# Expert weights in a ring of 20 pieces, a list of the used experts, and the first matrix in 2 MB transfers: a mixer and mixture-of-experts layer on one core

## The chip, the cores and the metric

The kernel runs on one core of a Trainium2 chip. The metric is the device time of one execution in microseconds (us).

## The reference, cut to what matters

One decoder layer with 512 tokens of width 1024, all in float32. A conditioning vector `c` gives shifts, scales and gates (`w_ada`, 24 MB). The first half of the layer (RG-LRU and pooling heads, `w_in`, `w_out`) gives `x1`. The second half is the mixture of 32 experts, of which each token uses four:

```python
logits = ht @ router_w + router_b
top_val, top_idx = lax.top_k(logits, TOP_K)          # 4 of 32
gates = jax.nn.softmax(top_val, axis=-1)
...
u = xb @ w1[e] + b1[e]                               # xb: the tokens of expert e; w1[e] is 1024 x 2048, 8 MB
y = clamped_swiglu(u) @ w2[e] + b2[e]                # w2[e] is 1024 x 1024, 4 MB
out = out.at[tok].add(y * wt)
```

Then a norm, a gate and the residual. Each used expert costs 12 MB of weights, however few tokens it has.

## The kernel before, in words

The kernel is written for each engine by hand, with semaphores between them. SyncE (SP) issues nearly all loads, ScalarE (ACT) activations and some loads, VectorE (DVE) arithmetic and routing, GpSimd (POOL) the gathers and scatters, TensorE (PE) the products.

**Head.** PE goes through `w_ada` in 24 pieces of 1 MB (`mod_piece`, L1253, three buffers; SP issues them in `load_ada`, L389), with the products of `w_in` (L1293) between them; SP issues the two 2 MB parts of `w_in` (`load_win`) and the 4 MB `w_out` between these pieces. Products with `w_out` are L1335.

**Routing.** DVE ranks the tokens by expert (`route_tile`, then L1074 to L1128) and writes `counts`, four rows of 32 integers in one partition: steps, halves, full steps, and 16 or 0 for whether the expert is loaded. PE makes the table of tokens (L1393). POOL gathers the first tokens from `h_rows` (L580), and PE turns them (L1406).

**Experts.** The tokens of an expert are worked on in halves of 32; a step is up to two halves. A matrix product with 32 tokens uses a quarter of the array's columns, four products at a time. For each expert PE makes the bias product (L1497), then for every half an up product over the 8 pieces of `w1` (`up`, L1418), turns the activations (L1427), then for every half a down product over the 4 pieces of `w2` (`down`, L1446). In the trace each product of float32 has two instructions, so a half's up product is x64 and its down product x32. The last pass over a piece counts up `w1_used` or `w2_used`; `u_ps` and `y_ps` say that the last piece is done.

**Weights.** `W1` has two slots of 8 pieces, `W2` one slot of 4; a piece is 1 MB, 8 KB in each of 128 partitions. SP loads `w1` of expert e into slot e modulo 2 as the up product of e - 2 frees its pieces (`load_w1`, L372). ACT loads `w2` of expert e as the down product of e - 1 frees them (`load_w2`, L377), on its own queue. Expert 0 is loaded ahead, `w1` of expert 1 once the counts are there. Every loop over experts goes over all 32 numbers in order: on PE as 16 rounds over a body written twice (L1485 to L1545). An expert without tokens is branched over (L1489, L1543) and its slot stays unused. In this input one expert has none: it is number 1.

**Tail.** When the last scatter is done (`moe_done`, L648) PE turns the gates (L1551) and multiplies by `b2` (L1563), SP loads the experts' results (`y_rows`, L483), and DVE sums them (L1214, L1217).

Of the kernel before, what the change touches and what calls it, by code (L numbers as in the profile page):

```python
# [5 lines left out]
def hybrid_layer(nc, x, c, w_ada, b_ada, norm_mix_pre, norm_mix_post, w_in, conv_w, conv_b, gate_a_w, gate_a_b,  # L6
# [32 lines left out]
    VECS = 72  # L39

# [9 lines left out]
    w1_v = expert_w1[0].rearrange("e (k p) n -> e p k n", p=P)  # L50
# [3 lines left out]
    with ctx:  # L54
# [10 lines left out]
        W1 = sb("W1", [P, 2, KT, F2])  # L65
        W2 = sb("W2", [P, J, 2, D])
# [29 lines left out]
        def flat(v):  # L96
            return v.rearrange("p a b -> p (a b)")
# [3 lines left out]
        w_out_sb = W2[:, :, :, :].rearrange("p c r n -> p (c r) n")  # L101
        HALF = KT // 2
        A_lo, A_hi = flat(W1[:, 0, 0:HALF, :]), flat(W1[:, 0, HALF:KT, :])
        B_lo, B_hi = flat(W1[:, 1, 0:HALF, :]), flat(W1[:, 1, HALF:KT, :])

# [75 lines left out]
        idx_n = take(NQ).bitcast(i32)  # L181

# [7 lines left out]
        sel_e = take(2, P)  # L190
# [7 lines left out]
        counts = OV[0:1, 6656 - 4 * E:6656].rearrange("p (a e) -> p a e", a=4).bitcast(i32)  # L198

        y_all = carver(flat(W1[:, 1, :, :]))(TT, TOPK, D)  # L200
        take = carver(flat(W1[:, 0, :, :]))
# [87 lines left out]
        w1_in = [sems(f"w1_in{s}_", KT) for s in range(2)]  # L289
        w2_in = sems("w2_in", J)  # L290
# [80 lines left out]
        def load_w1(sp, e, slot, k):  # L371
            sp.dma_start(W1[:, slot, k, :], w1_v[bass.ds(e, 1), :, k, :].rearrange("e p n -> p (e n)"))\  # L372
                .then_inc(w1_in[slot][k], 16)


        def load_w2(engine, e, c, experts=w2_v):
            engine.dma_start(W2[:, c, :, :].rearrange("p r n -> p (r n)"),  # L377
                             experts[bass.ds(e, 1), :, c, :].rearrange("e p n -> p (e n)")).then_inc(w2_in[c], 16)

        @block.sync  # L380
        def _(sp):
# [31 lines left out]
            for k in range(KT):  # L413
                load_w1(sp, 0, 0, k)
            sp.wait_ge(prod, number["mix", TT - 1, 1] + 1)
            for c in range(J):
                load_w2(sp, 0, c)
# [5 lines left out]
            for k in range(KT):  # L423
                sp.sem_inc(w1_in[1][k], 16)
            load = sp.value_load(counts[0:1, 3, 1:2], min_val=0, max_val=16)
            with sp.If(load > 0):
                for k in range(HALF):
                    load_w1(sp, 1, 1, k)
            sp.wait_ge(idx_ok, 1)
            with sp.If(load > 0):  # L430
                for k in range(HALF, KT):
                    load_w1(sp, 1, 1, k)
            step, landed = sp.alloc_register("sp_step"), [sp.alloc_register(f"sp_landed{v}") for v in range(2)]
            sp.reg_mov(step, 0)
            full = sp.alloc_register("sp_full")
            sp.reg_mov(full, 0)
            sp.reg_mov(landed[0], 16)
            sp.reg_mov(landed[1], 16)
            sp.reg_add(landed[1], landed[1], load)

            def add_steps(e):
                n_steps = sp.value_load(counts[0:1, 0, e], min_val=0, max_val=T // (2 * H))
                sp.reg_add(step, step, n_steps)
                n_full = sp.value_load(counts[0:1, 2, e], min_val=0, max_val=T // (2 * H))
                sp.reg_add(full, full, n_full)

            def all_up(s, f):

                sp.wait_ge(u_ps[0], s + 1)
                apart(sp)  # L450
                sp.wait_ge(u_ps[1], f + 1)
                apart(sp)
# [1138 lines left out]
```

## Time and profile before

| what | value |
|---|---|
| median of 3 runs | 1488.22 us (1486.9 to 1490.2) |
| the profiled execution | 1486.98 us |
| its span in the trace | 1485.2 us |
| PE busy | 1235.9 us, 83% |
| data moved | 462.84 MB, 312 GB/s over the span |
| granted TensorE clock, mean | 0.904 |

Times in the trace count from the span's start. PE is TensorE's products, PEld its weight loads, PEq and SPq are sequencers. In a view of windows a row has start and end, length, then for each engine its busy time and the number of its instructions, then the granted clock (1.00 is 2.4 GHz, 0.50 is 1.2 GHz), the share of the DMA engines' time in use, and GB/s; where it is made for one line, only that line's instructions are counted. In a timeline a row has start, length, engine, line and operation; in brackets stand the idle time before it and what ended it. A row of waits has who waited, for whom, us in total, times, longest. In the chain of waits a row has start, length and what ran.

### The profile page before, as it was taken

To read this page: it belongs to the slowest core of one execution; us is meant where nothing else is said; L and a number is where in the kernel's file an instruction comes from. 1 tells how busy PE (TensorE), PEld (TensorE's weight loads), DVE (VectorE), ACT (ScalarE), POOL (GpSimd) and SP (SyncE) were. 2 spreads that over 40 slices of the span, in tenths; PEclk is the share of its full clock that TensorE was granted. 3 is DMA by queue.
4 is the path that set the end of the run, shared out by engine and by line. 5 is a ranking of instruction groups with operands and counts; after the bars stand their busy time and mean duration, and the time that the engine had idled before them with its cause. 6 is when DMAs were issued, how large, how long until landed. Compare 5 with 4: busy or idle time off the path is not lost.

```text
span 1485.2 us, 28342 instructions
## 1 busy us (share of the span) xinstructions
PE 1235.9 (83%) x8843; PEld 419.1 (28%) x8844; DVE 412.6 (28%) x864; ACT 218.8 (15%) x482; POOL 277.9 (19%) x421
## 2 busy tenths in 40 slices
PE   4799996567998999967767999987799889989961
PEld 1334455211332333311112333321132223322320
DVE  3223344411232232221111222321122222222317
ACT  2106632000101111110100111110011001101101
POOL 3023001210222132211110221321021211211212
PEclk9799996787999999987868999997799999999975
DMA  9971514399459678899999980689998998899354
GB/s 323 394 269 53 216 46 198 130 416 387 186 193 422 282 316 328 363 420 420 421 420 419 419 347 10 249 355 419 402 404 363 420 421 328 326 421 421 142 213 185
DMA packets 77461, 462.84 MB, mean 312 GB/s; under 512 B 11924, under 2 KB 12052, under 8 KB 29312
## 3 DMA queue, kind: packets, MB, share of 16 engines
q1 hardware_dynamic: 49280, 314.72, 52.1%
q10 hardware_dynamic: 17568, 126.14, 20.5%
q0 software_dynamic: 10592, 21.72, 4.3%
q8 instruction: 11, 0.18, 0.1%
q14 instruction: 10, 0.08, 0.0%
HBM read 453.08 MB, written 16.91 MB: 316 GB/s over the span
## 4 chain that ended last, share of the span: by engine, by line
PE 67%; DMA 15%; DVE 6%; SPq 5%; ACT 3%; issue 3%; POOLq 1%; ACTq 1%; POOL 0%; DVEq 0%
PE bank L1418 33%; PE bank L1446 18%; DMA W<-in_expert_w 12%; SPq L372 4%; PE bank L1293 4%; PE bank L1335 4%; PE bank L1427 2%; DMA W<-in_w_ada 2%; PE bank L1497 2%; PE bank L1253 1%; PE bank L1406 1%; DVE W L1217 1%; DVE OV L1139 1%; DMA OV<-h_rows,src_cur 1%; DMA W<-y_rows 1%
## 5 line engine op out<-in xcount | busy, mean ns | idle before, releaser
L1418 PE MATMUL bank<-W,OV 128*32 128x512 f32 x5056 | 576.9, 609 | 49.4 <-DMA W<-in_expert_w 49.4
L1446 PE MATMUL bank<-W,OV 128*32 128x512 f32 x2528 | 320.4, 652 | 44.7 <-ACT OV L798 22.1
L1418 PEld LDWEIGHTS bank<-W,OV 128*32 128x32 f32 x5056 | 157.2, 111 | 443.3 <-issue 364.9
L1139 DVE TENSOR_TENSOR OV<-bank,OV 128x512 f32<-128x512 f32 x79 | 54.7, 692 | 489.3 <-PE bank L1418 483.8
L1446 PEld LDWEIGHTS bank<-W,OV 128*32 128x32 f32 x2528 | 83.0, 117 | 227.6 <-issue 191.5
L1152 DVE COPY OV<-bank 64x512 f32<-64x512 f32 x79 | 54.8, 693 | 298.4 <-PE bank L1446 296.1
L580 POOL DMA_INDIRECT OV<-h_rows,src_cur x104 | 106.6, 1025 | 61.8 <-POOL src_cur L575 42.7
L575 POOL COPY src_cur<-OV 128x2 int32 (+1 forms) x52 | 11.5, 222 | 523.3 <-PE bank L1406 493.6
L793 ACT ACTIVATE OV<-OV 128x256 f32<-128x256 f32 x79 | 35.3, 447 | 467.1 <-DVE OV L1141 453.7
L1427 PE MATMUL bank<-ident,store 128*128 128x128 f32 x216 | 49.0, 316 | 48.2 <-DVE store L1147 47.3
L1293 PE MATMUL bank<-W 128*128 128x512 f32 x192 | 86.1, 602 | 0.0
L798 ACT ACTIVATE OV<-bank 128x256 f32<-128x256 f32 x108 | 40.6, 386 | 204.1 <-PE bank L1427 199.6
L1427 PEld LDWEIGHTS bank<-ident,store 128*128 128x128 f32 x216 | 33.4, 205 | 91.9 <-issue 91.8
L1156 DVE TENSOR_TENSOR OV<-bank,OV 64x512 f32<-64x512 f32 x79 | 53.9, 683 | 19.0 <-DMA y_rows<-OV,dst_cur_a 9.8
L1335 PE MATMUL bank<-W,OV 128*128 128x512 f32 x128 | 56.2, 594 | 0.9 <-issue 0.9
L590 POOL DMA_INDIRECT y_rows<-OV,dst_cur_a x51 | 47.5, 930 | 47.7 <-POOL dst_cur_a L586 41.1
L821 ACT ACTIVATE OV<-bank 128x512 f32<-128x512 f32 x31 | 18.5, 598 | 248.6 <-issue 155.8
L789 ACT ACTIVATE OV<-bank 128x256 f32<-128x256 f32 x102 | 35.9, 374 | 122.9 <-PE bank L1406 122.9
L1293 PEld LDWEIGHTS bank<-W 128*128 128x128 f32 x192 | 36.4, 193 | 49.3 <-issue 48.9
L586 POOL COPY dst_cur_a<-OV 64x1 int32 (+1 forms) x51 | 9.2, 180 | 209.2 <-DVE OV L1156 209.2
L1406 PE MATMUL bank<-ident,OV 128*128 128x128 f32 x204 | 34.8, 295 | 12.2 <-DMA OV<-h_rows,src_cur 12.2
L1497 PE MATMUL bank<-b_all,OV 128*128 128x512 f32 x62 | 39.1, 717 | 6.8 <-issue 6.8
(231 smaller groups left out, 681.7 us busy)
## 6 DMA issues: line engine op xcount, KB each, us to landing
W<-in_expert_w SPq DMA_DIRECT2D x252, 1024.0 KB, 16.9
W<-in_expert_w ACTq DMA_DIRECT2D x120, 1024.0 KB
W<-in_w_ada SPq DMA_DIRECT2D x24, 1024.0 KB, 8.4
W<-y_rows SPq DMA_DIRECT2D x4, 2048.0 KB, 14.6
W<-in_w_in SPq DMA_DIRECT2D x3, 2048.0 KB, 11.8
W<-in_w_out SPq DMA_DIRECT2D x1, 4096.0 KB, 25.0
store<-in_x SPq DMA_DIRECT2D x4, 512.0 KB, 5.2
h_rows<-W POOLq DMA_DIRECT2D x4, 512.0 KB, 3.3
```

Of the source, the lines that this page charges most:

```text
L372: sp.dma_start(W1[:, slot, k, :], w1_v[bass.ds(e, 1), :, k, :].rearrange("e p n -> p (e n)"))\
L580: pool.indirect_dma_start(xg[hf], None, h_rows, bass.IndirectOffsetOnAxis(ap=src_cur[:, hf:hf + 1], axis=0), bounds_check=T * J - 1, oob_i ...
L1139: TTo(u_sb[:, hf, :], bank[hf][:, :], b1_cur, ALU.add).then_inc(u_ok[hf], 1)
L1152: nc.vector.tensor_copy(y_part[hf], bank[4 + hf][YP:2 * YP, :]).then_inc(y_part_ok, 1)
L1156: TTo(y_sb[hf], bank[4 + hf][0:YP, :], y_part[hf], ALU.add).then_inc(y_ok[hf], 1)
L1293: last = mm(ps[:, :], win_ring[:, slot, k, f * P:(f + 1) * P], hT[:, k, :], start=(k == 0), stop=(k == KT - 1))
L1335: last = mm(ps[:, :], catT[:, k, i * P:(i + 1) * P], w_out_sb[:, k, n * 512:(n + 1) * 512], start=(k == FT), stop=(k == FT - 1))
L1406: last = tr(bank[2][:, at:at + P], xg[hf][:, m * P:(m + 1) * P], ident[:, :])
L1418: last = mm(bank[hf][H * j:H * j + H, :], xT[:, hf, k % QM, H * (k // QM):H * (k // QM) + H], W1[:, slot, k, UW * j:UW * j + UW], start=(k ...
L1427: last = tr(gT_bank[hf][:, r * P:(r + 1) * P], act_store[:, hf, r::2], ident[:, :])
L1446: last = mm(bank[4 + hf][H * j:H * j + H, :], gT[:, hf, r, H * c:H * c + H], W2[:, c, r, HW * piece:HW * piece + HW], start=(c == 0), stop ...
L1497: mm(b1_bank[:, :], sel_e[:, slot, :], b1_all[:, :], start=True, stop=True).then_inc(b1_ps, 1)
```

## The change

The two buffers become one, `W`, of the same size: five groups of four pieces. The expert at place i of a list takes groups 3i, 3i + 1 and 3i + 2, modulo 5: two for `w1`, one for `w2`. A piece is refilled when the piece that stood in it five groups earlier is used up. All weights are now loaded by SP, in the order in which PE uses them; ACT loads none.

The list holds the experts that have tokens (and expert 0), in order, 36 places. PE, DVE and SP work it out before the table of tokens is made: a product counts each expert's tokens, another gives its place, two more write halves and numbers by place into `counts`. POOL, ACT and DVE go over the places one by one. PE and SP go over them in 7 rounds of a body written five times, so their last round ends with places that hold no expert.

`w1` is read with two neighbouring rows per partition, 16 KB at a time, in four transfers of 2 MB in place of eight of 1 MB; a transfer waits for both of its pieces to be free, and PE waits for both to be there. The turn of the tokens (L1406) reads every second element to match.

Three smaller things: in the head the 4 MB of `w_out` are loaded after the last piece of `w_ada`, and the second part of `w_in` after three more pieces; ACT makes the sigmoid of `c` before the squares of `x`; DVE makes the bias selector of the next expert after this one's activations.

```diff
+    GROUPS = 5
+    NPOS = E + J
+    LAPS = 7
-    w1_v = expert_w1[0].rearrange("e (k p) n -> e p k n", p=P)
+    w1_v = expert_w1[0].rearrange("e (c p r) n -> e p c (r n)", p=P, r=2)
-        W1 = sb("W1", [P, 2, KT, F2])
-        W2 = sb("W2", [P, J, 2, D])
+        W = sb("W", [P, GROUPS, J, F2])
...
+        def load_w1(sp, e, g, k):
+
+            sp.dma_start(W[:, g, k % J:k % J + 2, :].rearrange("p r n -> p (r n)"),
+                         w1_v[bass.ds(e, 1), :, k // 2, :].rearrange("e p n -> p (e n)")).then_inc(w_in_at[g][k % J], 16)
+            sp.sem_inc(w_in_at[g][k % J + 1], 16)
...
+            return [(3 * u + part) % GROUPS for part in range(3)]
...
-            load_win(2, 1)
             for n in range(2 * PIECES, 2 * PIECES + ADA_RING):
                 load_ada(n)
-            sp.dma_start(w_out_sb, w_out_v).then_inc(wout_in, 16)
+            load_win(2, 1)
...
+            sp.dma_start(w_out_sb, w_out_v).then_inc(wout_in, 16)
...
+            def first_matrix(e, u, uses):
+
+                g = groups_of(u)
...
+                for k in range(0, KT, 2):
+                    part, c = k // J, k % J
+                    landed_there(g[part], c, uses[part])
+                    landed_there(g[part], c + 1, uses[part])
+                    if k + 1 < J - 1:
+                        after_up(s, k + 1 + J)
+                    elif k + 1 == J - 1:
+                        after_all(u_ps, s, f)
+                    elif c + 1 < J - 1:
+                        sp.wait_ge(w2_used, (J - 1) * s + (c + 2))
+                        apart(sp)
+                    else:
+                        after_all(y_ps, s, f)
+                    load_w1(sp, e, g[part], k)
...
+                for c in range(J):
+                    landed_there(g, c, uses[2])
+                    after_up(s, c)
+                    load_w2(sp, e, g, c)
...
+            with sp.Fori(1, LAPS) as lap:
...
+                for u in range(GROUPS):
+                    i = GROUPS * lap + u
+                    add_steps(bass.ds(i - 2, 1))
+                    with sp.If(steps_of(i) > 0):
+                        e = expert_at(i)
...
-                with act.If(load > 0):
...
-                        load_w2(act, e, part, w2_v[1:E])
...
+            for b in range(TT):
+                last = mm(bank[6][0:E, 0:1], sel[:, b, :], ones[:, 0:1], start=(b == 0), stop=(b == TT - 1))
+            last.then_inc(halves_ok, 1)
...
-                        last = tr(bank[2][:, at:at + P], xg[hf][:, m * P:(m + 1) * P], ident[:, :])
+                        last = tr(bank[2][:, at:at + P], xg[hf][:, m::QM], ident[:, :])
...
-            with pe.Fori(0, E // 2) as pair:
-                for slot in range(2):
-                    e = 2 * pair + slot
+            with pe.Fori(0, LAPS) as lap:
+                for v in range(3):
+                    pe.reg_mov(landed[v], 48 * lap + 16 * (v + 1))
+                for u in range(GROUPS):
+                    e = GROUPS * lap + u
```

## Rows read from the trace of the kernel before

**Rows 1.** The page, busy time and the span in 40 slices.
```profile
PE 1235.9 (83%) x8843; PEld 419.1 (28%) x8844; DVE 412.6 (28%) x864; ACT 218.8 (15%) x482; POOL 277.9 (19%) x421
...
DMA  9971514399459678899999980689998998899354
GB/s 323 394 269 53 216 46 198 130 416 387 186 193 422 282 316 328 363 420 420 421 420 419 419 347 10 249 355 419 402 404 363 420 421 328 326 421 421 142 213 185
```

**Rows 2.** Waits of PE, longest in total first.
```profile
PE bank L1418 <- DMA W<-in_expert_w: 49.4, 20, 4.2
...
PE bank L1446 <- DMA W<-in_expert_w: 17.7, 7, 4.0
...
PE bank L1497 <- issue: 6.8, 1, 6.8
```

**Rows 3.** Windows of single experts, instructions of L1418 alone (x64 is one half).
```profile
280.04:306.66 26.62, 8.24 (x64) 2.04 (x64) 0.82 0.81 324
...
426.49:462.94 36.45, 21.01 (x192) 6.03 (x192) 1.00 0.79 323
...
491.99:551.14 59.15, 34.95 (x320) 10.09 (x320) 1.00 0.67 269
...
867.53:972.10 104.57, 62.84 (x576) 18.21 (x576) 1.00 0.42 165
972.10:989.49 17.39, 7.07 (x64) 1.98 (x64) 0.90 1.01 420
...
1162.47:1191.69 29.22, 14.15 (x128) 3.96 (x128) 0.94 1.01 421
...
1221.06:1267.66 46.60, 28.09 (x256) 8.01 (x256) 1.00 0.84 344
```

**Rows 4.** Windows of three stretches of experts, all engines.
```profile
280.00:427.00 147.00, 118.80 (x921) 35.02 (x920) 30.78 (x65) 14.23 (x38) 27.39 (x41) 0.88 0.75 302
624.00:831.00 207.00, 149.59 (x1035) 40.91 (x1031) 36.53 (x77) 17.43 (x45) 30.53 (x47) 0.81 1.01 420
972.10:1096.60 124.50, 98.57 (x723) 27.71 (x719) 24.64 (x53) 11.77 (x30) 19.94 (x30) 0.84 1.00 414
```

**Rows 5.** Timeline of PE where expert 1 is branched over.
```profile
306.66 2.07 PE L1497 MATMUL bank<-b_all,OV 128*128 128x512 f32 x2 [6.81 <-issue]
```

**Rows 6.** Window of the tail, where rows of 16 KB are loaded.
```profile
1446.00:1454.00 8.00, 7.19 (x9) 2.29 (x7) 7.70 (x8) 1.15 (x2) 0.00 (x0) 0.50 1.00 428
```

**Rows 7.** The page, DMA queues and issues.
```profile
q8 instruction: 11, 0.18, 0.1%
...
W<-in_expert_w SPq DMA_DIRECT2D x252, 1024.0 KB, 16.9
```

**Rows 8.** Window of one expert of three halves, all engines.
```profile
426.49:462.94 36.45, 34.90 (x310) 11.50 (x306) 10.59 (x22) 4.39 (x12) 8.42 (x14) 1.00 0.79 323
```

**Rows 9.** Timeline of the tail.
```profile
1426.62 0.69 DVE L1152 COPY OV<-bank 64x512 f32<-64x512 f32 x1 [6.93 <-PE bank L1446]
...
1438.08 1.03 PE L1551 MATMUL bank<-ident,G 128*32 128x128 f32 x4 [11.52 <-POOLq L648]
...
1446.09 1.53 DVE L1214 SCALAR_TENSOR_TENSOR W<-W,gates,bank 128x512 f32<-128x512 f32 x2 [17.95 <-DMA W<-y_rows]
```

**Rows 10.** Timeline of the head, PE at piece 12 of w_ada.
```profile
68.67 1.94 PE L1253 MATMUL bank<-W 128*32 128x512 f32 x8 [6.23 <-DMA W<-in_w_ada]
```

**Rows 11.** Timeline of DVE in the routing.
```profile
255.13 0.18 DVE L1075 TENSOR_SCALAR OV<-OV 128x32 int32<-128x32 int32 x1
```

**Rows 12.** The chain of waits, two gathers.
```profile
276.26 2.83 DMA OV<-h_rows,src_cur
...
846.67 7.58 DMA OV<-h_rows,src_cur
```

**Rows 13.** Weight loads of PE's transposes, by line: ns shortest, median, longest.
```profile
L1406 PEld LDWEIGHTS bank<-ident,OV x204: 137/140/231, 279.1 to 1417.4; 128*128 128x128 f32 x102
L1427 PEld LDWEIGHTS bank<-ident,store x216: 194/205/223, 292.7 to 1419.9; 128*128 128x128 f32 x108
```

More of the change, by code:

```diff
@@ L181, in hybrid_layer @@
         idx_n = take(NQ).bitcast(i32)
+        take = carver(W[:, 4, :, :].rearrange("p k n -> p (k n)")[:, KT * FT * P + 3 * D:])
+        by_expert = take(8)
+        by_expert_i = take(2).bitcast(i32)
+        place = take(NPOS)
+        iota_id = take(1)
         take = carver(OV)
@@ L189, in hybrid_layer @@
         y_sb = [take(HW)[0:YP], take(HW)[0:YP]]
-        sel_e = take(2, P)
+        sel_e = take(P)
         b1_cur = take(UW)
@@ L369, in linker, with load_w2, groups_of, uses_of @@
             return link
[L371 to L378, printed above, removed]
+        def load_w1(sp, e, g, k):
+            sp.dma_start(W[:, g, k % J:k % J + 2, :].rearrange("p r n -> p (r n)"),
+                         w1_v[bass.ds(e, 1), :, k // 2, :].rearrange("e p n -> p (e n)")).then_inc(w_in_at[g][k % J], 16)
+            sp.sem_inc(w_in_at[g][k % J + 1], 16)
+        def load_w2(sp, e, g, c):
+            sp.dma_start(W[:, g, c, :], w2_v[bass.ds(e, 1), :, c, :].rearrange("e p n -> p (e n)"))\
+                .then_inc(w_in_at[g][c], 16)
+        def groups_of(u):
+            return [(3 * u + part) % GROUPS for part in range(3)]
+        def uses_of(u):
+            return [(3 * u + part) // GROUPS for part in range(3)]
         @block.sync
@@ L441, in add_steps @@
-            def add_steps(e):
-                n_steps = sp.value_load(counts[0:1, 0, e], min_val=0, max_val=T // (2 * H))
+                e = expert_at(1)
+                for k in range(J, KT, 2):
+                    load_w1(sp, e, 4, k)
+            step, full, step_next = [sp.alloc_register(f"sp_{v}") for v in ("step", "full", "step_next")]
+            for reg in (step, full):
+                sp.reg_mov(reg, 0)
+            landed = [sp.alloc_register(f"sp_landed{v}") for v in range(3)]
@@ new lines, in after_up, with after_all, landed_there, add_steps @@
+            def after_up(s, k):
+                sp.wait_ge(w1_used, (KT - 1) * s + (k + 1))
+                apart(sp)
+            def after_all(signals, s, f):
+                sp.wait_ge(signals[0], s + 1)
+                apart(sp)
+                sp.wait_ge(signals[1], f + 1)
+                apart(sp)
+            def landed_there(g, c, use):
+                if use is not None:
+                    sp.wait_ge(w_in_at[g][c], use)
+                    apart(sp)
+            def add_steps(i):
+                n_steps = sp.value_load(counts[0:1, 0, i], min_val=0, max_val=T // (2 * H))
@@ L1388, in _ @@
             pe.wait_ge(sel_ok, TT)
+            for b in range(TT):
+                last = mm(bank[6][0:E, 0:1], sel[:, b, :], ones[:, 0:1], start=(b == 0), stop=(b == TT - 1))
+            last.then_inc(halves_ok, 1)
             total_add(TT - 1).then_inc(rank_ok, 1)
             rank_add(TT - 1, TT - 1).then_inc(rank_ok, 1)
+            pe.wait_ge(used_ok, 1)
+            mm(bank[6][0:E, 1:2], upper[0:E, 0:E], by_expert[0:E, 2:3], start=True, stop=True).then_inc(pos_ok, 1)
+            pe.wait_ge(place_ok, 1)
+            for v in range(2):
+                last = mm(bank[6][0:1, 64 + 64 * v:64 + 64 * v + NPOS], by_expert[0:E, v:v + 1], place[0:E, :], start=True,
+                          stop=True)
+            last.then_inc(list_ok, 1)
+            pe.wait_ge(counts_ok, 1)
             for n in range(TK):
@@ L1434, in turn_first, with down @@
                 pe.reg_add(turned, turned, 1)
-            def down(hf, n, tiles, frees, arrived=None):
+            def down(hf, n, u, tiles, frees, arrived=None):
                 if 0 in tiles:
@@ L1496, in _ @@
                         pe.wait_ge(sel_e_ok, e + 1)
-                        mm(b1_bank[:, :], sel_e[:, slot, :], b1_all[:, :], start=True, stop=True).then_inc(b1_ps, 1)
+                        mm(b1_bank[:, :], sel_e, b1_all[:, :], start=True, stop=True).then_inc(b1_ps, 1)
                         with pe.If(n_full > 0):
```

221 lines of the change are left out of this document (105 added, 116 removed).

## The prediction, made before the change was run

> **What bounds the kernel now.** The page comes first: PE is busy 83% of the span, but the slices show two regimes in the experts' part. In most slices from 30% of the span on, the DMA row reads 9 and 420 GB/s, and those are the slices in which PE drops to 5 to 7; around them PE reads 9 while the DMA row falls to 4, 1 or 0 [rows 1]. So neither resource is the bound throughout. The waits say what PE lacks in the first kind: weights, in front of the up products and in front of the down products [rows 2].
>
> How much that costs, I read from windows cut at the bias product that opens each expert. Without a wait an expert takes 17.4 us with one half, 29.2 with two, 36.45 with three, 46.6 with four, 59.15 with five and 104.6 with nine [rows 3]; seven halves, of which there is one expert, lie midway between the last two, 81.9. Its 12 transfers of 1.049 MB take 12 x 2.50 = 30.0 us at 420 GB/s. Experts of one or two halves eat faster than the DMA feeds, the others slower. The 31 used experts have, in order, 1 1 7 3 2 5 3 3 1 2 1 1 1 1 3 3 9 1 1 1 4 2 3 2 2 4 3 2 2 4 1 halves (the x of such windows over 64). Three stretches [rows 4] lose time: the first three experts take 147.0 us where 17.4 + 17.4 + 81.9 = 116.7 would do (30.3 lost); the run 1 2 1 1 1 1 3 takes 207.0 for 152.6 (54.4 lost); 1 1 1 4 takes 124.5 for 98.8 (25.7 lost). The other 17 experts lose nothing, so a change to loading can win at most these 110 us.
>
> **The ring.** Both kernels hold 20 pieces. Before, the room that an expert leaves is filled with the first matrix of the expert after next, while the second matrix of the next one starts only when the last down product frees its slot, and shares the DMA with it. After, pieces come in the order of use. What is left of each loss is then a sum over bytes.
> Run of seven, from 624.0: the ring is full, up to `w1` of the second expert. Before the last expert's first pass can end, 4 + 4 x 12 + 8 = 60 pieces must come, 149.8 us, from the moment the first four are used (1.1 + 3.4 us) and with some 2 us to land and 1.7 us for the last pair of products: 158. Unhindered, PE would be there at 116.2 + 8.0 = 124.2. Lost: 34; I take 36 for bubbles between used and refilled, and win 18.
> 1 1 1 4, from 972.1: 4 + 12 + 8 = 24 pieces, 59.9 + 4.5 + 2 + 1.7 = 68.1, against 52.2 + 8.0 = 60.2. Lost 8, taken as 9: I win 17.
> First stretch: 6.8 us are PE's idle time at the jump over expert 1 [rows 5], which the list removes; 2.4 us are the half clock of the first expert (26.62 - 6.81 - 17.39) [rows 3], which stay. The rest is that `w1` of the second and third used expert is asked for only from the first up product on, since expert 1's slot stands empty. With the list the second's comes at routing time; the third's 8 pieces and the second's `w2` need 30 us from about the first up pass, and PE needs them after 37. I leave 7 us of loss and win 23.
>
> **16 KB rows.** The rate with 8 KB rows is 420 in every saturated window [rows 3, 4]; the loads of 16 KB rows in the tail run at 428 [rows 6]. Then the 40 pieces of `w1` among the 60 save 40 x 0.05 = 2 us. The price is that two pieces are waited for together, 2.5 us at a time, inside my allowance for bubbles. Bounds 0 and 4; I take the row's 2. Loading now takes 8 issues an expert, not 12 [rows 7], all on SP; they cost SP nothing that PE waits for, since SP queues far ahead of landing (16.9 us median) [rows 7].
> The Trainium skill, in DMA: Bandwidth & Descriptors, Specifications, asks for no more than 512 B per piece for line rate, so by it this term is 0; the 428 of the tail speaks mildly against that.
> Sum of ring, list and rows: 18 + 17 + 23 + 2 = **60 us won**.
>
> **The longer code.** This is what the change pays with. All of PE's code came once: 11 blocks, 0.18 MB, 16 KB each, on the instruction queue [rows 7], though the loop over two bodies ran 16 times; so two bodies stay where they are. The one place where PE left a body at its start for the next costs 6.8 us of idle PE, put down to no engine and no weight [rows 5]; I read it as code that had to be fetched. One pass through a body is 616 products and weight loads [rows 8] and some registers and waits. The loop is now five bodies, over 3000 instructions, and ends with a branch back over all of them, at places 5, 10, 15, 20, 25 and 30. The trace does not show a branch so far back: from 0 (the loop still stays) to 6.8 us each, as for the only far branch there is. I take 6.8, since it is the same engine and kind. At places 10 and 20 PE is about to wait for weights anyway, which covers it; four count: **+27 us**.
> The Trainium skill gives a rule for this, in Runtime: NRT & Kernel Launch, Instruction fetch mechanics: PE's instruction memory holds 2048 instructions, filled in order in blocks of 256, and a taken branch out of it waits for a fetch. By it two bodies fit and five do not. The trace agrees as far as it goes, with blocks of 16 KB and none fetched again.
> **The tail.** Places 31 to 34 hold no expert, so PE makes four jumps over a body after the last down product. That is 4 x 6.8 = 27 us at full price. PE is free at 1426.6 and needed at 1438.1, and what it makes there is read 8 us later by a DVE that waits for `y_rows` [rows 9], of which about 2 us are slack: 27 - 13.5 = 13.5 at most, 0 if a jump costs up to 3.4. The DMA is half idle there, so I take +5. SP passes the same places long before, while it has nothing to load.
>
> **The head and the routing.** PE idles 6.2 us for a piece of `w_ada` that stands in SP's queue behind the 4 MB of `w_out` [rows 10]. These move behind the last piece, well before they are used: -6.2. The squares of `x` come a few us later; PE's own waits for `w_ada` cover that, and if not, up to 4 us come back. DVE has 13 new small operations and 7 old ones less before the table, 0.2 us each [rows 11]: +1.3, with PE's replies +2. The first gather took 2.8 us on an idle DMA; one under load took 7.6 [rows 12], and now `w1` of place 1 is loading beside it: +4.8. On ACT the waits in front of the `w2` loads vanish, which frees nothing PE waits for. SP's single queue means that a `w2` piece not yet free holds up the `w1` behind it, but that is needed later.
> **The turn with stride 2.** The weight load of L1427, which reads every second element, takes 205 ns, that of L1406 140 [rows 13]. All 204 would make 13 us if nothing covered them; they overlap products, so I take +2 (bounds 0 and 13).
>
> **Sum.** -60 - 6.2 + 2 + 4.8 + 2 + 27 + 5 = -25. The profiled execution took 1486.98 us (span 1485.2), 1.2 below the median of the runs; its own time less 25 is 1462.
>
> **The rivals.**
> *A, as forecast, 0.50:* 1462.
> *B, the code costs nothing, 0.28:* the far branches are met by fetches made ahead. Then the 27 and the 5 go: 1430. For it: the jump is PE's only wait for issue in front of L1497 [rows 2], so 15 branches back over two bodies cost nothing. Against it: five bodies were never in a loop here.
> *C, slower, 0.14:* the code is fetched all the time and the branches inside a body miss too: an expert of one half jumps over the pair's part, some 300 of the instructions, one of two halves over the odd half's. In the 21 experts that are not covered by weight waits, a miss costs 6.8 us. All other terms and the tail leave 1487 - 52 = 1435, so eight misses in all give the gain back; four are the laps, and four more decide. With ten of them it is 1462 + 68 = 1530.
> *D, the change does not do what it says, 0.05:* the order of the pieces was not what cost, only their bytes and the missing list. Then the 35 us of the two later stretches stay: 1497.
> The rest, 0.03, is for prices that I have not seen.
>
> **Range and chances.** B and A must be inside, and the part of C with a few misses: 1424 to 1490. About 0.2% (3 us) is what a measurement of this kernel can tell from no change. Faster: A and B with part of the rest, 0.81; within 0.2%: 0.03; slower: C and D, 0.16.
>
> **What would show it.** The bias product of the third place starts some 38 us after the first, with no gap in front of the second. In the run of seven, PE's waits for weights stand only in front of up products, at its end, and none in front of L1446. 3 to 8 us of idle PE, put down to issue, stand in front of L1497 at every fifth place, and the instruction queue has far more than 11 blocks. L1551 starts later than 11.5 us after the last down product. The saturated rate is 423 or more. It is wrong if the instruction queue stays near 11 blocks (B), if issue gaps stand inside the bodies (C), or if the 207 us stay over 200 (D).

## The result, and the profile after

The changed kernel takes 1497.6 us (median, 1496.5 to 1498.7) against 1488.4 of the kernel before on the same chip: 1.0054 of it, with an interval of 1.0037 to 1.0072. On another chip, below, it is 1.0025 [1.0013, 1.0037]. It is slower; the forecast was 1462 with a range of 1424 to 1490, and 1497.6 lies outside it. The profiled execution's span is 1496.9 us, 11.7 more than before.

The page of the changed kernel, DMA row of the slices and queues, answers to [rows 1, 7]:
```profile
DMA  9882515894688478999999924599999968897252
GB/s 318 307 298 107 232 54 234 350 423 190 268 350 359 172 279 359 425 421 422 421 424 422 411 114 180 194 420 424 422 424 411 421 278 350 356 421 317 91 231 116
...
q1 hardware_dynamic: 48704, 440.55, 71.5%
...
q8 instruction: 107, 1.75, 0.5%
```
Most of the saturated slices read 420 to 425 GB/s, hardly more than before. The instruction queue (packets, MB, share) has moved 107 blocks where there were 11 [rows 7].

Waits of PE in the changed kernel (total us, times, longest), against [rows 2]:
```profile
PE bank L1570 <- issue: 31.4, 6, 6.3
PE bank L1624 <- issue: 24.9, 1, 24.9
...
PE bank L1498 <- DMA W<-in_expert_w: 18.7, 8, 3.3
PE bank L1486 <- DMA OV<-h_rows,src_cur: 17.5, 3, 15.7
PE bank L1498 <- issue: 17.3, 7, 3.9
```
L1498 is the up product (L1418 before), L1526 the down product (L1446), L1570 the bias product that opens an expert (L1497), L1624 PE's first work in the tail (L1551). The waits for weights have fallen from 67.1 us to 18.7, and none stands in front of a down product. In their place are 73.6 us of waits for nothing that the profile shows, in three places: in front of the bias product six times, in front of the first up product seven times (six experts of one half, 1.9 to 3.9 us each, and 0.4 us at one of two halves), and once in the tail.

Windows of the three stretches, as [rows 4] (all engines, columns as there), and then the timeline of PE at two branches back, one inside the run of seven and one at its end:
```profile
277.50:399.80 122.30, 111.39 (x920) 36.10 (x918) 30.40 (x64) 14.23 (x38) 25.64 (x40) 0.96 0.73 296
608.50:816.60 208.10, 151.25 (x1034) 44.43 (x1030) 37.86 (x79) 17.60 (x45) 31.55 (x49) 0.86 1.01 422
962.00:1078.30 116.30, 94.80 (x722) 29.25 (x718) 24.57 (x52) 11.75 (x30) 19.62 (x30) 0.90 1.00 419
```
```profile
661.02 2.07 PE L1570 MATMUL bank<-b_all,OV 128*128 128x512 f32 x2 [5.84 <-issue]
666.67 8.82 PE L1498 MATMUL bank<-W,OV 128*32 128x512 f32 x64 [3.58 <-issue]
...
816.65 1.74 PE L1570 MATMUL bank<-b_all,OV 128*128 128x512 f32 x2 [4.59 <-issue]
```
The first stretch went from 147.0 to 122.3 us, the last from 124.5 to 116.3. The run of seven, the largest of the three, takes 208.1 where it took 207.0. The other 17 experts, which lost nothing before, take 702.6 us instead of 668.1.

Waits are not all of that. These are the sums over the windows of the 17 experts, cut at their bias products, in the changed kernel and then in the kernel before (length, then busy time by engine):
```profile
sum 702.47, PE 649.00 PEld 205.53 DVE 185.89 ACT 78.92 POOL 140.80; mean PE 216.33 PEld 68.51 DVE 61.96 ACT 26.31 POOL 46.93
```
```profile
sum 668.63, PE 630.57 PEld 200.77 DVE 187.35 ACT 78.94 POOL 143.36; mean PE 210.19 PEld 66.92 DVE 62.45 ACT 26.31 POOL 47.79
```
PE is idle for 15 us more, and its products take 18 us more. The next windows show where: 8 us behind the branch back at place 5, where PE had been idle for 6.3 us, and then the start of the same expert before:
```profile
473.27:477.27 4.00, 4.00 (x14) 1.10 (x18) 0.00 (x0) 0.60 (x1) 0.00 (x0) 0.50 1.00 416
477.27:481.27 4.00, 4.00 (x32) 1.00 (x28) 0.00 (x0) 0.00 (x0) 0.00 (x0) 0.77 0.88 373
```
```profile
491.99:495.99 4.00, 4.00 (x34) 1.23 (x34) 1.75 (x3) 0.00 (x0) 1.10 (x2) 1.00 1.00 416
```
The granted clock behind the wait is 0.50 and then 0.77, where it was 1.00, and this expert of five halves takes 62.2 us instead of 59.15, the wait in front of it not counted.

The tail of the changed kernel, timeline, against [rows 9]:
```profile
1423.13 3.64 PE L1526 MATMUL bank<-W,OV 128*32 128x512 f32 x32 [1.23 <-ACT OV L870]
1451.63 1.01 PE L1624 MATMUL bank<-ident,G 128*32 128x128 f32 x4 [24.86 <-issue]
...
1457.70 1.53 DVE L1283 SCALAR_TENSOR_TENSOR W<-W,gates,bank 128x512 f32<-128x512 f32 x2 [26.33 <-PE bank L1636]
```
PE is away for 24.9 us after its last down product, where 11.5 were covered, and DVE now waits for PE (before it waited for `y_rows`): the tail is 70.1 us, not 58.6. A second thing has moved there. SP's load of `x1` for the tail, in the changed kernel and then in the kernel before:
```profile
1427.30 0.41 SPq L550 DMA_DIRECT2D W<-x_rows  x1
```
```profile
1393.64 0.40 SPq L479 DMA_DIRECT2D W<-x_rows  x1
```
It used to be done before the last results were scattered; now it is issued 2.3 us ahead of the last scatter. From the start of that scatter to the release of `y_rows` it takes 13.6 us, not 8.7.

| part | forecast, us | measured, us |
|---|---|---|
| head and routing | +0.6 | -2.5 |
| first stretch | -23 | -24.7 |
| run of seven (order and rows) | -20 | +1.1 |
| 1 1 1 4 | -17 | -8.2 |
| other 17 experts (code, turn) | +29 | +34.5 |
| tail | +5 | +11.5 |
| sum | -25 | +11.7 |

### The profile page after: what moved, and what is told of

The parts are those of the page before. It is cut to its first block, busy times and chain, and to the rows that moved or that the text cites. A ratio compares the mean times of both kernels' runs of the same rounds, so it can differ in the third digit from the quotient of the medians.

```text
span 1496.9 us, 28081 instructions
## 1 busy us (share of the span) xinstructions
PE 1242.8 (83%) x8857; PEld 428.8 (29%) x8858; DVE 413.5 (28%) x870; ACT 217.4 (15%) x481; POOL 274.9 (18%) x422
## 4 chain that ended last, share of the span: by engine, by line
PE 74%; DMA 8%; DVE 7%; issue 6%; ACT 3%; SPq 1%; POOLq 1%; POOL 0%; DVEq 0%; ACTq 0%
PE bank L1498 37%; PE bank L1526 19%; DMA W<-in_expert_w 5%; PE bank L1362 4%; PE bank L1404 4%; PE bank L1507 2%; PE bank L1570 2%; DMA W<-in_w_ada 2%; PE bank L1322 1%; PE bank L1486 1%; DVE OV L1202 1%; DVE W L1286 1%; SPq L383 1%; DMA OV<-h_rows,src_cur 1%; DMA y_rows<-OV,dst_cur_a 1%
## 5 line engine op out<-in xcount | busy, mean ns | idle before, releaser
L1498 PE MATMUL bank<-W,OV 128*32 128x512 f32 x5056 | 579.5, 612 | 36.0 <-DMA W<-in_expert_w 18.7
L1526 PE MATMUL bank<-W,OV 128*32 128x512 f32 x2528 | 321.1, 654 | 26.1 <-ACT OV L870 20.3
L1498 PEld LDWEIGHTS bank<-W,OV 128*32 128x32 f32 x5056 | 162.0, 113 | 429.9 <-issue 401.3
L1526 PEld LDWEIGHTS bank<-W,OV 128*32 128x32 f32 x2528 | 84.8, 118 | 210.0 <-issue 203.5
L870 ACT ACTIVATE OV<-bank 128x256 f32<-128x256 f32 x108 | 40.7, 386 | 210.3 <-PE bank L1507 207.9
L1570 PE MATMUL bank<-b_all,OV 128*128 128x512 f32 x62 | 40.1, 732 | 31.4 <-issue 31.4
L1486 PE MATMUL bank<-ident,OV 128*128 128x128 f32 x204 | 38.5, 312 | 17.5 <-DMA OV<-h_rows,src_cur 17.5
## 6 DMA issues: line engine op xcount, KB each, us to landing
W<-in_expert_w SPq DMA_DIRECT2D x124, 1024.0 KB, 16.5
```

The lines of the kernel that those rows point to most:

```text
L1486: last = tr(bank[2][:, at:at + P], xg[hf][:, m::QM], ident[:, :])
L1498: last = mm(bank[hf][H * j:H * j + H, :], xT[:, hf, k % QM, H * (k // QM):H * (k // QM) + H], W[:, groups_of(u)[k // J], k % J, UW * j:UW ...
L1526: last = mm(bank[4 + hf][H * j:H * j + H, :], gT[:, hf, r, H * c:H * c + H], W[:, groups_of(u)[2], c, D * r + HW * piece:D * r + HW * piec ...
L1570: mm(b1_bank[:, :], sel_e, b1_all[:, :], start=True, stop=True).then_inc(b1_ps, 1)
```

## The experiments

Three theories stood at the start. One: the longer code of PE costs what it seems to, and the list and the head carry nearly all of the gain, the ring next to nothing. Two: the ring itself holds loads back. Three, which I thought least of: the size of the rows matters.

**The list alone.** The kernel before, with its two slots and PE loop of two bodies, but the experts in use packed to the front:
```diff
-                load = sp.value_load(counts[0:1, 3, bass.ds(e, 1)], min_val=0, max_val=16)
-                with sp.If(load > 0):
+                with sp.If(steps_of(bass.ds(e, 1)) > 0):
+                        ex = expert_at(bass.ds(e, 1))
...
-                            load_w1(sp, e, slot, k)
+                            load_w1(sp, ex, slot, k)
```


> The kernel before with the list of used experts alone: two slots for w1, one for w2, 1 MB pieces, a PE loop of two bodies, no change to the head. My theory (the list is what repairs the first stretch, the ring adds little): the first three experts fall from 147 to 122 to 125 us, the later stretches stay at 207 and 124.5, the start of the first expert moves from 280.0 to about 283.5 (longer routing and a first gather beside the loads). Sum -24 + 3.5 = 1468 us. Rival (the first stretch was won by the ring's order of loads, not by the list): it stays near 140 and the time near 1485. The instruction queue should stay near 11 blocks and the 6.8 us of idle PE in front of L1497 should be gone or at the end.

**List and head.** The same, with the changed order of loads and of ACT's work ahead of the experts.
```diff
-            load_win(2, 1)
             for n in range(2 * PIECES, 2 * PIECES + ADA_RING):
                 load_ada(n)
-            sp.dma_start(w_out_sb, w_out_v).then_inc(wout_in, 16)
+            load_win(2, 1)
```


> The same with the changed order in the head (w_out after the last piece of w_ada, the second part of w_in later, the sigmoid of c first). Theory: the first expert starts 6 us earlier than with the list alone, as 6.2 us of idle PE at a piece of w_ada vanish: 1462 us. Rival: the head gains nothing, as the waits move to another piece: 1468 us.

Measured: 0.9905 [0.988, 0.993] of the kernel before (1474.6 us) with the list, 0.9848 [0.9831, 0.9866] (1467.8) with list and head. Windows of the second kernel:
```profile
276.46:405.33 128.87, 114.70 (x919) 35.64 (x918) 30.09 (x63) 14.25 (x38) 26.06 (x40) 0.93 0.72 286
603.23:810.61 207.38, 150.06 (x1034) 40.70 (x1031) 37.07 (x77) 17.39 (x45) 30.52 (x47) 0.80 1.01 420
951.71:1076.46 124.75, 98.34 (x722) 27.58 (x718) 24.74 (x53) 11.74 (x30) 19.99 (x30) 0.85 1.00 414
```
The list gives 18 of the first stretch's 25 us (147.0 to 128.9; 127.6 with the list alone), the head and routing 3.6 (first expert at 276.46, not 280.04). The later stretches stay as they were, 207.4 and 124.8 us, as expected. Both kernels came out some 6 us above the times expected of them (1474.6 for 1468, 1467.8 for 1462); the head's own share is 6.8 us for 6. These two parts of the change alone are worth 1.5%, so the rest of it costs 1.7 to 2.1% (1.0054 / 0.9848 = 1.021; on the chip where both were measured, below, 1.0025 / 0.986 = 1.017).

**Four bodies.** The kernel before, with PE's loop body written four times, nothing else:
```diff
-            with pe.Fori(0, E // 2) as pair:
-                for slot in range(2):
-                    e = 2 * pair + slot
+            with pe.Fori(0, E // 4) as pair:
+                for turn_no in range(4):
+                    slot = turn_no % 2
+                    e = 4 * pair + turn_no
```


> The kernel before with PE's loop over the experts written four times in a row (8 rounds of 4 in place of 16 of 2), nothing else changed: same loads, same order, same products. Theory (the cost is PE's code fetched again each round): the instruction queue goes from 11 to about 90 blocks, idle PE put down to issue stands where the loop goes back, 5 to 10 us at each of 7 branches of which 5 are outside the stretches that wait for weights: 1488 + 25 to 50 = 1513 to 1538 us. Rival (the issue waits of the changed kernel come from the ring's waits and registers, not from the length of the code): 1488 us and 11 blocks.

Measured: 1.0241 [1.0218, 1.0264], 1527.5 us. Its instruction queue, and waits of PE (L1418 and L1446 are the up and down products as before, L1498 is here the bias product):
```profile
q8 instruction: 100, 1.64, 0.4%
```
```profile
PE bank L1418 <- issue: 25.5, 9, 4.8
PE bank L1498 <- issue: 14.4, 4, 5.7
PE bank L1446 <- issue: 7.8, 4, 3.2
```
Same work, same loads, same order; the same products are put through a loop of four bodies instead of two, and the 11 blocks become 100. The kernel loses 36 us. PE idles for 2.8 to 5.7 us at each of the seven branches back. The profile puts three of these waits down to nothing and four, 4.3 to 4.6 us, to DVE L1160, the bias selector; the kernel before has no wait there, and nothing but PE's loop was changed. This shows that length of code in the loop costs time by itself.

**The last two places behind the loop.** The changed kernel, with places 30 and 31 written once more behind a loop of six laps, so that PE does not jump over places 32 to 34 and needs no far branch for place 30.
```diff
-            with pe.Fori(0, LAPS) as lap:
+            with pe.Fori(0, LAPS - 1) as lap:
...
+            for u in range(2):
+                one_place(LAPS - 1, u)
```


> The changed kernel with the last two places written after the loop on PE (6 rounds of 5 bodies, then 2 bodies), so that one place without an expert is passed in place of four, and one branch back less is made. Theory: the 24.9 us that PE idles before the gates are turned fall to 11.5, the tail is again 58 to 60 us, and the branch at place 30 costs nothing: 1497.6 - 11.5 - 5 = 1481 us. Rival (passing over code is not what holds the tail, the loads of x1 and y_rows are): 1494 us or more.

Measured: 0.9947 [0.993, 0.9963], 1483.2 us, where the whole change has 1.0054 and 1.0025: 12 to 16 us less, where 16.5 were expected. Its tail, timeline of PE (L1526 is the last down product, L1631 the first work behind it):
```profile
1414.67 4.99 PE L1526 MATMUL bank<-W,OV 128*32 128x512 f32 x32 [1.22 <-ACT OV L870]
1435.15 1.03 PE L1631 MATMUL bank<-ident,G 128*32 128x128 f32 x4 [15.48 <-POOLq L720]
```
PE is again waiting for POOL's queue there, not for itself. The tail takes 62.5 us: code was 7.6 of the 11.5 us that it had grown by. The other 3.9 stay, since POOL's queue is released 12.6 us after the last scatter begins; the load of `x1` beside that scatter, which is still late here, fits this, but no run took it away. The branch back behind place 29, with the slower products after it, was worth the other 7 us.

**Rows of 8 KB in the ring,** and the changed kernel beside it, on one chip. The transposes of the gathered tokens go back to consecutive columns with it.
```diff
-    w1_v = expert_w1[0].rearrange("e (c p r) n -> e p c (r n)", p=P, r=2)
+    w1_v = expert_w1[0].rearrange("e (k p) n -> e p k n", p=P)
...
-                        last = tr(bank[2][:, at:at + P], xg[hf][:, m::QM], ident[:, :])
+                        last = tr(bank[2][:, at:at + P], xg[hf][:, m * P:(m + 1) * P], ident[:, :])
```


> The changed kernel with its first matrix back in 1 MB transfers of 8 KB rows (pieces of 128 consecutive rows, transposes of the gathered tokens by consecutive columns); ring, list and head order as changed. Theory (the ring's PE code costs what was lost, the size of the rows nothing): the stretch of seven experts stays at 208 us for its 81 pieces (2.56 us each), the time within 2 us of the changed kernel's 1497.6, ratio to the kernel before 1.002 to 1.008. Rival 1 (16 KB rows bring some of the 425 to 428 GB/s seen at the tail): each piece 0.04 to 0.07 us dearer, so that the byte-bound stretches (some 170 pieces) grow by 7 to 12 us: 1504 to 1509, ratio 1.010 to 1.014. Rival 2 (2 MB transfers hold back the pieces behind them, by up to a piece at each wait): the stretches get shorter by 3 to 6 us: 1492 to 1495, ratio 1.000 to 1.003.

> The changed kernel itself, once more, as the reference for the run without 16 KB rows on the same chip: ratio to the kernel before 1.004 to 1.007 under every theory; anything else is the spread between chips.

Measured: 0.9973 [0.9958, 0.9988] with 8 KB rows, 1.0025 [1.0013, 1.0037] with 16 KB. My theory (no difference) and the first rival (slower without them) both fall: the 16 KB rows and the turn that goes with them cost 8.6 us (1483.9 against 1475.3). The second rival had the sign, but expected it in the stretches bound by bytes, and about half of it. The run of seven is the same in both, 207.9 and 208.0; the difference builds up outside it. In the profiled executions the third expert starts 3.1 us later with 16 KB rows, 4.0 more come up to the last expert's end, and 2.7 in the tail. The rate in the run of seven does rise with 16 KB rows, from 418 to 422 GB/s. Part of the 8.6 us is the turn with stride 2, which this run takes back as well: place 16, with nine halves and five turns, takes 104.94 us with it and 104.56 without. That is 0.08 us a turn, by my estimate at most 4 us over all 51. PE's waits for gathered tokens, without and with 16 KB rows:
```profile
PE bank L1483 <- DMA OV<-h_rows,src_cur: 15.0, 2, 14.6
```
```profile
PE bank L1486 <- DMA OV<-h_rows,src_cur: 18.3, 4, 15.6
```

**16 KB rows in two slots,** on the list-and-head kernel (with the turn of stride 2 that goes with them), and that kernel again beside it.
```diff
-            sp.dma_start(W1[:, slot, k, :], w1_v[bass.ds(e, 1), :, k, :].rearrange("e p n -> p (e n)"))\
-                .then_inc(w1_in[slot][k], 16)
+            sp.dma_start(W1[:, slot, k:k + 2, :].rearrange("p r n -> p (r n)"),
+                         w1_v[bass.ds(e, 1), :, k // 2, :].rearrange("e p n -> p (e n)")).then_inc(w1_in[slot][k], 16)
+            sp.sem_inc(w1_in[slot][k + 1], 16)
```


> The kernel before with the list of used experts and the changed order of loads in the head (the run of 0.985 of before), and now the first matrix in 2 MB transfers of 16 KB row pairs, in its two slots as before. Theory (the size of the rows is worth nothing, as pieces cost 2.56 us with either): 0.985 of the kernel before, 1466 to 1470 us at before 1490; the stretch of seven experts 207 to 209 us. Rival 1 (faster transfers): 5 to 12 us less, 0.977 to 0.981. Rival 2 (a 2 MB transfer waits for two free pieces and lands as one, so that the stall of each byte-bound expert grows by up to one piece of 2.5 us; 9 such experts): 5 to 20 us more, 0.988 to 0.998.

> The kernel before with the list of used experts and the changed order of loads in the head, once more, as the reference for the run that adds 16 KB rows to it on the same chip: 0.983 to 0.987 of the kernel before.

Measured: 1.0111 [1.0091, 1.0131] against 0.986 [0.9841, 0.9879]: 36 us lost, more than any theory had. Here the two matrices come on two queues, the first by SP (q1), the second by ACT (q10). Waits of PE with 16 KB rows, and then with 8 KB rows:
```profile
PE bank L1491 <- DMA W<-in_expert_w: 91.3, 21, 6.4
```
```profile
PE bank L1462 <- DMA W<-in_expert_w: 39.6, 14, 4.4
...
PE bank L1490 <- DMA W<-in_expert_w: 24.1, 10, 4.2
```
L1491 and L1490 are the down products: with big rows PE waits for no weights but the second matrix. The queues in a window in which PE waits for a piece of it (635.6 to 642.9 us with 16 KB rows, 617.6 to 622.5 with 8 KB; packets, MB, share):
```profile
q1 hardware_dynamic: 143, 2.08, 67.1%
q10 hardware_dynamic: 143, 1.04, 34.1%
```
```profile
q10 hardware_dynamic: 143, 1.04, 51.0%
q1 hardware_dynamic: 140, 1.02, 49.7%
```
Both queues move the same number of packets, whatever a row holds. A packet is one row (2.08 MB are 127 rows of 16 KB), but for 16 of 4 bytes that came beside them here. So doubling the first matrix's row takes the second matrix's share from a half to a third, at the moment at which PE needs it. Down products that wait for it start 7.4 us apart (635.59, 642.97) instead of 5.0 (617.54, 622.56). A piece alone takes 2.56 us (207.4 us for the 81 pieces that land in the run of seven); times 3 and times 2 that is 7.7 and 5.1.

**4 KB rows,** to test this from the other side: each 1 MB piece of the first matrix in two transfers.
```diff
+            for n in range(2):
+                part = slice(n * F2 // 2, (n + 1) * F2 // 2)
+                sp.dma_start(W1[:, slot, k, part], w1_v[bass.ds(e, 1), :, k, part].rearrange("e p n -> p (e n)"))\
+                    .then_inc(w1_in[slot][k], 16)
```


> The kernel before with the list of used experts and the changed head, and each 1 MB piece of the first matrix in two transfers of 4 KB rows (8 KB before, 16 KB in the run at 1.011). New theory, from that run (pieces of the second matrix, on ACT's queue, came 5.5 to 5.9 us apart where TensorE waited for them, against 3.9 to 4.2 with 8 KB rows; 2.56 us is a piece alone): two queues share the engines row by row, so a queue with 16 KB rows has 16/(16 + r) of the rate against rows of r KB: 5.1, 3.8 and now 3.2 us for a piece of the second matrix. So its waits fall from 3.9 to about 3.2 us apart, the first matrix's rise, the stretch of seven experts stays at 208 to 210 us (its bytes are the same), places 1, 18 and 28 give back 3 to 8 us in all: 0.980 to 0.985 of the kernel before. Rival 1 (what hurt was that a 2 MB transfer waits for two free pieces, not its share): waits for the second matrix stay at 3.9 to 4.2 us, 0.984 to 0.988. Rival 2 (4 KB rows are moved slower): the seven experts take over 212 us, 0.99 or more.

The figures in that text take the second matrix's rows for 16 KB, and "5.5 to 5.9 us apart" are the lengths of waits, not distances; its rows are 8 KB (1.04 MB in 143 packets, above). With that the rule gives 8/(8 + r): a third, a half, and now two thirds, a piece each 3.8 us. Measured queues from 657.8 to 661.5 us, and waits:
```profile
q10 hardware_dynamic: 141, 1.02, 66.8%
q1 hardware_dynamic: 142, 0.52, 35.0%
```
```profile
PE bank L1464 <- DMA W<-in_expert_w: 58.8, 20, 6.7
...
PE bank L1492 <- DMA W<-in_expert_w: 5.4, 5, 2.4
```
Two thirds, and down products 3.8 us apart (657.77, 661.59). The waits for the second matrix are nearly gone and stand in front of the first. The first rival falls: the waits did not stay. The ratio is 0.9851 [0.9832, 0.9869], no change from 0.985 and 0.986: what the second matrix gains the first loses (64 us of waits in all, as with 8 KB rows). The second rival holds as well, a little: the seven experts take 214.3 us at 412 GB/s, not 207.4 and 209.3 (on two chips) at 420.

The Trainium skill, in DMA: Bandwidth & Descriptors, Queues, rings and completion order, says that an engine takes turns between the queues it has work for, a whole packet of descriptors from each. The equal counts of rows above agree with it, if packets hold equally many rows; what one turn holds no run here shows.

**Another order of experts.** What is left in the list-and-head kernel over its unstalled lengths is 94 us, nearly all of it at or next to experts of one or two halves. So the list alternates: expert 0, then most halves, fewest, most, fewest.
```diff
+            link(TS(is_before, key, by(4), None, ALU.is_lt))
+            link(nc.vector.reduce_sum(by(6), is_before, axis=AX.X))
...
+            link(STT(by(3), by(6), 2.0, by(7), ALU.mult, ALU.min))
```


> The kernel before with the list of used experts and the changed head, and with the list in another order: expert 0, then the experts with most halves and those with fewest in turn (0, 9 halves, 1, 7, 1, 5, 1, 4 and so on), worked out on the chip by some 18 more small operations of DVE and one more product (3 to 5 us). Theory (what is left over the unstalled lengths, 94 us, is the weights' time of neighbouring one-half experts, 12 pieces of 2.56 us against 17.4 us of products, and goes wherever an expert of four or more halves stands beside each): unstalled lengths 1036 us; a pair of 3 and 1 halves is still short by 61.4 - 53.9 = 7.5 us, four of these, pairs of 2 and 2 by 3 us each, so 30 to 40 us of stalls stay: 1400 to 1420 us, ratio 0.94 to 0.955. Rival 1 (the stalls come from the two slots' coupling, that the first matrix of the next expert but one may only follow the products of this one, and come back with every small expert): 60 to 90 us stay, 1440 to 1475, 0.965 to 0.99. Rival 2 (TensorE without its pauses is granted less clock, so the products get longer): the stretch of long experts runs at 0.85 or less where it has 0.91 now, 1430 to 1460.

Measured: 0.9607 [0.9591, 0.9623], 1431 us, with 55 us left: between theory and first rival, as the second matrix, at half the rate, is late in the seven one-half experts from place 8 on. TensorE's granted clock over all experts was 0.95, so the second rival (less clock) falls. With 4 KB rows:

> The alternating order of experts (0.961 of the kernel before, 55 us over the unstalled lengths, most of it waits of 3 to 5 us for the second matrix in one-half experts at places 8 to 20) with 4 KB rows for the first matrix. Theory (shares by row): the second matrix has 4/5 instead of 2/3 of the rate, its waits fall by a quarter to a half, 10 to 15 us of the 55: 0.950 to 0.955. Rival (the stall is set by the bytes of a pair of experts, whichever matrix comes first): the waits move to the first matrix, 0.958 to 0.963.

Measured: 0.9543 [0.9524, 0.9562], 1422.8 us (45 us left). The ratio is the one expected, but the shares in that text are not: by the rule as corrected above the second matrix goes from a half to two thirds. Its waits fall by 70%, and the rival has its part too, since new waits stand in front of the first matrix. Waits of PE for weights, 8 KB rows (L1512 is the down product) and then 4 KB rows (L1514 the down, L1486 the up product):
```profile
PE bank L1512 <- DMA W<-in_expert_w: 36.7, 12, 4.7
```
```profile
PE bank L1486 <- DMA W<-in_expert_w: 21.8, 7, 6.7
...
PE bank L1514 <- DMA W<-in_expert_w: 10.7, 7, 2.9
```
This is the fastest version here, 4.6% under the kernel before, with PE's loop of two bodies and 11 blocks of code. The step from 0.9607 was measured on another chip; two kernels that were measured on two chips differed by 0.001 and 0.003.

**The ring in that order.** The changed kernel with 8 KB rows, the last two places behind the loop, and the alternating list.

> The changed kernel with 8 KB rows, with the last two places written behind TensorE's loop, and with the alternating order of experts: what the ring is worth where its pieces come in one queue and in the order of use. Theory: the waits for the second matrix go (one queue, no share to lose); left are four pairs of 3 and 1 halves that are short by up to 7.5 us each and five branches back at 5 to 6 us, part of which the loads use to catch up: 40 to 60 us over the unstalled lengths, 1415 to 1435 us at before 1490, ratio 0.95 to 0.963, no clear gain over the two slots in the same order (0.961). Rival 1 (code waits add in full to the bytes): 65 us or more, 0.965 or more. Rival 2 (the deeper ring hides the bytes of all small experts): 30 us of code alone, under 0.945.

Measured: 0.9812 [0.9791, 0.9833], 1462.3 us; the first rival. Waits of PE:
```profile
PE bank L1517 <- issue: 24.4, 8, 4.1
PE bank L1586 <- issue: 24.2, 5, 5.8
...
PE bank L1545 <- issue: 4.6, 4, 1.6
```
No wait for weights is left at all. Of the 79 us left over the unstalled lengths, 53 are the waits above. L1586 is the bias product, at each of the five branches back; L1517 is the first up product of an expert of one half, behind the jump over the pair's part of its body, at eight of them. The two slots in the same order, with 37 us of waits for the second matrix and none for a branch, are 31 us faster (0.9607 against 0.9812). What the ring would be worth with PE code that stays in place, no run shows.

## Why the prediction was wrong, step by step

The direction was wrong, and by the table the miss of 37 us has four parts.

*"The ring is full, up to `w1` of the second expert", at 2.50 us a piece* is the largest, 21 us with the rows' 2. Counted from the DMA records, 110.6 pieces had landed when place 8 began, where a full ring means 116; it was 110.8 before the change. So 65.4 pieces were still to come before the last expert's first pass, not 60. And over the run of seven both kernels land 81 pieces, 81.2 in 208.1 us and 81.0 in 207.0, 2.56 us each, since gathers and results share the engines (1.049 MB at 420 GB/s alone are the 2.50). So the stretch is bound by its bytes from its first microsecond: 65.4 x 2.56 and the 3.7 us for landing and products make 171 us. The order did bring the last expert's first pass forward, from 178.5 to 173 us after the start, not to 158, and the branch back behind it (4.59 us) took most of that. For 1 1 1 4, 8.2 of 17 us came, for the same reason: 220 pieces had landed at its start where 224 are a full ring, so 28 were to come, not 24.

*Rows of 16 KB, "bounds 0 and 4; I take the row's 2"* had the sign wrong: they cost 8.6 us together with the turn, shown by undoing both; I had put the two together at nothing. The row behind it, 428 GB/s in the tail [rows 6], was a rate of a queue alone. The rate did rise (418 to 422 GB/s), and it did not pay; in the two slots, what counted was who else wants the engines. That the cost in the ring, too, is the share of other queues is only partly shown: waits for gathers, on POOL's queue, grew by 3.3 us, and the loading of pieces in pairs may hold back the rest. It stays open.

*The longer code* had the right mechanism and even the right row, the 6.8 us at one far branch [rows 5], but only its idle time, and not all of that. PE idles at all six branches back (5.2 us on average). And jumps inside a body miss as well, 17.3 us in all, most of it at six experts of one half. In the 17 experts that the term was for, this is 15.9 us at three branches back (places 5, 25 and 30) and 1.9 at a jump. What I put at nothing is the clock behind a wait: at place 5, products that ran at 1.00 ran at 0.50 and 0.77 for 8 us. The turns are some 2 us of the 18 us of longer products there (31 turns at 0.08, an estimate); the rest goes with granted clocks of 0.97, 0.98 and 0.94 over the three parts, where they were 0.99, 1.00 and 0.97. The trace of before had shown it, in the first 4 us behind the jump over expert 1:
```profile
306.66:310.66 4.00, 4.00 (x14) 1.09 (x18) 0.00 (x0) 0.60 (x1) 0.00 (x0) 0.50 1.02 421
```
That expert of one half took 20.45 us, not 17.4, the 6.8 us in front of it not counted. I had put the jumps inside a body into rival C as a condition, at 6.8 us each, and given it 0.14; in truth the idle time of both kinds was less than that, and the lower clock came on top. Together with the turn the 17 experts lost 34.5 us instead of 29. The Trainium skill's rule in Runtime: NRT & Kernel Launch, Instruction fetch mechanics, 2048 instructions in blocks of 256, would set the limit between the two bodies that stay and the four that do not; the runs with two, four and five bodies agree (11, 100 and 107 blocks). The same section also speaks of a window of two blocks, out of which a taken branch waits for a fetch; two bodies are over 1232 instructions, and their 11 blocks speak against that window for PE.

*The tail, "13.5 at most ... I take +5"* measured +11.5. Its bound held, and the choice inside it had no row: the four jumps came to 24.9 us, 6.2 each, close to the row's 6.8. The last two places behind the loop take 7.6 of it back; the late load of `x1` was not in the sum at all.

*First stretch* (-24.7 for -23) was right, and *head* (-2.5 for +0.6) nearly so. The list gives 18 to 19 of the first, as the two runs without the ring show. The head's order gives 7.3 us at the first expert (283.75 to 276.46) for 6.2 forecast, and the longer routing with its gather costs 3.7 for 6.8.

*Rival D* gave 1497, the measured time, by half of its mechanism: the order of pieces was worth nothing in the run of seven, but 8 us in the other stretch; the rest of that number is dearer code, so that it fits is luck. Of the signs listed, those of the forecast for code and tail were there, and those of C (waits inside the bodies) and D (the run of seven over 200 us) as well; the rate stayed at 422 GB/s in the run of seven, under the 423.

## What to carry over

Before an order of loads is costed, count what has landed at the start of a byte-bound stretch; if all the bytes needed take the stretch's length, reorder the work, not the loads. A loop on an engine pays for its unrolling as soon as its bodies no longer stay in instruction memory, at every branch back and at many jumps over a large part, in idle time and then in clock, so look at the instruction queue's blocks first. With two queues sharing the engines, the row size of each is its weight: give the longer rows to what is needed first. Where bytes bind, this only moves the wait (0.985 stayed 0.985); in the alternating order it went with a gain (0.961 to 0.954).

## What the hardware showed that I had not expected

- Two queues that both have work move equally many packets: 143 and 140 with rows of 8 KB, 143 and 143 with 16 and 8 KB, 142 and 141 with 4 and 8 KB.
- PE's loop of two bodies is fetched once (11 blocks in all); of four bodies, 100 blocks and 36 us.
- Rows of 4 KB on one of two queues bring the rate from 420 to 412 GB/s, 2 to 3% longer in a byte-bound stretch.
- Behind 6.3 us of idle PE the granted clock was 0.50 for 4 us and 0.77 for the next 4. With fewer waits it was higher, 0.95 over all experts in the fastest version, where the kernel before had 0.92.
- The same change measured 1.0054 and 1.0025 on two chips, whose times for the kernel before were 1488 and 1480 us. I had expected 1.004 to 1.007 on the second.
